# One encoder block on one core: rows of the first expert pair found by one-hot tables, expert weights loaded during the mix product, and more of the gated embedding inside the expert loop

## The chip, the core and the metric

The kernel runs on one core of a Trainium2 chip. The core has TensorE (PE in the profile, with its weight loads as PEld), VectorE (DVE), ScalarE (ACT), GpSimd (POOL) and SyncE (SP), and 16 DMA engines that all queues share. Time is device microseconds of one launch. One matrix product is meant by "product" below; "turned" means transposed on TensorE.

## What is computed

One transformer-like block over 512 tokens of width 1024, all in float32:

```python
h = _layernorm(x, ln0_w, ln0_b)
proj = h @ w_in[i]                       # q, k, v, z, xBC, dt, two gates
ya = _window_attention(...) @ w_out_attn[i]
ys = _ssd(...) @ w_out_ssd[i]
mix = (gates[:, :, 0, :] * ya + gates[:, :, 1, :] * ys) @ w_out[i]
h1 = _layernorm(DN_ALPHA * h + mix, ln1_w[i], ln1_b[i])
moe = _hier_moe(h1, ...)                 # 32 experts, the best 2 of the best group of 8
ple = jax.nn.sigmoid(h1 @ w_ple_gate[i] + b_ple_gate[i]) * (p[i] @ w_ple[i])
h = _layernorm(DN_ALPHA * h1 + moe + ple, ln2_w[i], ln2_b[i])
```

Every token goes to two experts with two weights. One expert is `silu(t @ w_gate) * (t @ w_up)`, weighted, times `w_down`; its three matrices have 1 MB each, so the 32 experts have 96 MB of weights. `ple` is the gated embedding.

## The kernel before

**Programs.** Each engine has one hand-written program, and semaphores join them; each engine does its work strictly in the order written. `link(...)` on VectorE makes the next instruction wait for the one before. `psum_plan` is a list of the units of work that need a PSUM bank, in TensorE's order; it gives each unit the next bank and the semaphore value at which the unit before in that bank has been read. `opened(key)` on TensorE is that wait. `plan_last` is the wait for all banks before the expert loop.

**Up to the expert loop.** The mix product (L1081) makes 8 bank-sized results in 55 us; VectorE adds and normalises each of the four token tiles (L1888, L1557 to L1572) and ScalarE scales them into `base`. TensorE turns `h1` (L1104) and makes the router's logits (L1096). VectorE picks group, two experts and their weights, then `sel` (which expert each token takes) and `upto` (running sums over the tiles). Meanwhile TensorE makes units of the gated embedding.

**The gated embedding** has 16 units `n` (four column slices by four token tiles). `ple_gate` is 8 accumulated products (L1125), `ple_in` two more (L1131). VectorE adds the bias (`ple_sum`, L1949), ScalarE takes the tanh (L1468), VectorE multiplies and adds to `base` (`ple_out`, L1956 and L1961). The first `EARLY` = 10 units come ahead of the loop, the other six in the loop, one for two pairs from pair 2 on, half a unit in each pair. ScalarE copies the turned rows of pair 0 behind the tanh of unit 8.

**The ranks and the rows.** Behind unit 1 TensorE sums `sel` to each token's rank within its expert (L1158 to L1160). From rank and count VectorE makes the row number of each choice (experts have 64 rows in order; what is over 64 goes to further rows, by a scan over the experts, L1990 and L1991) and then control words of the loop over full experts (L2013 to L2019), and storeU. POOL waits for the row numbers, scatters (weight, token) pairs to `row_info` in DRAM by 8 indirect DMAs (L769), loads the whole table back into `info` (L774), and then gathers the token rows of pair 0 and pair 1 (`rows_fetched`, L781).

**The expert loop.** 16 pairs of experts, 128 rows each (64 to an expert). For pair p TensorE does in this order: `gate_up` (L1180), turning of the rows of pair p+1 (L1145, ScalarE copies them), half of an embedding unit, `act_t` (L1205, ScalarE copies), the second part of the unit, `down` (L1195). ScalarE and VectorE copy the result to `eout`, and POOL scatters it to `y_rows` in DRAM (L801). There are two buffers `xg` for gathered rows, `xg[p % 2]`; POOL issues the gather of pair p+2 ahead of the scatter of pair p, which puts it right behind the scatter of pair p-1. The weights lie in a ring of 12 slots of 1 MB: slots 0 to 5 for even pairs, 6 to 11 for odd ones, each six being gate, up, down of one expert and then of the other. SP loads gate and up of pair p+2 when `gate_up` of pair p is done (L630), and down when `down` of pair p is done (L642).

**SP's order ahead of the loop.** After the second output product it loads one slice of the embedding's gate, then waits for the end of the mix product (`s_pe_mix`), and only then loads `w_ple`, all six slots of pair 0, stores `h1` to DRAM (L654), loads gate and up of pair 1, two more slices of the embedding gate (L617) and down of pair 1. `MOE_FREED` says for each slot which event frees it: the mix product for slots 0, 1, 8, 9, and the second output product (`s_pe_ys`, or `s_ys_read`) for the other eight.

**The end.** With pair 14's results in DRAM, POOL gathers each token's two rows with an adding DMA (L811), pair 15 is added by a product from chip memory (L1218), and VectorE, ScalarE and POOL normalise and store.

Of the kernel before, what the change touches and what calls it, by code (L numbers as in the profile page):

```python
# [113 lines left out]
EARLY = 10  # L114
LATE_FROM = 2
NO_TOKEN = 4 * ROWS

# [6 lines left out]
def psum_plan(sems):  # L124
# [89 lines left out]
    for n in range(EARLY):  # L214
        if n == EARLY - 1:
            for b in range(2):
                unit(("xf", b), 1, ("xgT_sb", b + 1))
        unit(("pl", n), 1, ("pp_read", n + 1))
        if n == RANKS_AFTER:
            unit("rk", 1, ("rk_read", 1))  # L220
# [15 lines left out]
    last = {}  # L236
    for b in range(8):
        for s, v in holder[b]:
            last[s.name] = (s, max(v, last.get(s.name, (s, 0))[1]))
    return place, list(last.values())  # L240


def block_kernel(nc, aps, out):
    with ExitStack() as ctx:
# [104 lines left out]
        xg = [shaped(R_A + 3072 + D * b, "p (k n) -> p k n", k=KD, n=P) for b in range(2)]  # L349
        xgT = [shaped(r, "p (k t) -> p k t", k=KD, t=P) for r in (R_X, R_A)]  # L350
        eactT = shaped(R_A + 1024, "p (b k t) -> p b k t", b=2, k=2, t=P)
        eout = shaped(R_Y, "p (b n) -> p b n", b=2, n=D)
# [42 lines left out]
        for c in range(2):  # L395
            rv[8 + c] = token_info[:, :, c, 0].bitcast(F32)
        storeU = ctx.enter_context(nc.sbuf_tensor("storeU", [P, PAIRS], U32))
        rowsU = ctx.enter_context(nc.sbuf_tensor("rowsU", [P, 2 * NT], U32))
        ctl = ctx.enter_context(nc.sbuf_tensor("ctl", [P, EXTRA + 2], I32))
# [37 lines left out]
        s_h1_ready = sem("h1_ready")  # L437
        s_h1_st = sem("h1_st")
# [62 lines left out]
        s_rk_read = sem("rk_read")  # L501
# [39 lines left out]
            s_rk_read, s_rt_read, s_sc_read, s_seg_read, s_st_read, s_xt_read, s_yT_read, s_ya_read,  # L541
# [6 lines left out]
        xg_in = [sem(f"xg_in{b}") for b in range(2)]  # L548
        plan, plan_last = psum_plan(sems)
# [43 lines left out]
        def _(sp):  # L593
# [25 lines left out]
            def gate_up_weights(p):  # L619

                for half in range(2):
                    for w, t in ((0, wg), (1, wu)):
# [4 lines left out]
                        elif half == w == 0:  # L627
                            sp.wait_ge(s_gu_mm, p - 1)
                        src = t[p * 2 + half].rearrange("(p k) f -> p k f", p=P)
                        sp.dma_start(ring[:, slot], src).then_inc(slot_in[slot], 16)  # L630

            def down_weights(p):

                for half in range(2):
                    slot = expert_slot(p % 2, half, 2)
# [50 lines left out]
        def _(pool):  # L686
# [90 lines left out]
            def rows_fetched(p):  # L777

                if p >= 2:
                    pool.wait_ge(s_xT_mm, 2 * (p - 1))  # L780
# [1366 lines left out]
```

## Time and profile before

| | |
|---|---|
| median of 3 runs | 821.24 us (820.75 to 822.28) |
| the profiled execution's own time | 820.64 us |
| its span in the trace | 818.6 us |
| TensorE busy / weight loads | 739.7 us (90%) / 499.5 us (61%) |
| VectorE, ScalarE, GpSimd busy | 403.5, 191.0, 162.2 us |
| DMA | 172.55 MB, 211 GB/s over the span |
| chain that ended last | PE 63%, DMA 23%, DVE 8% |

Times in the trace count from the span's start. A busy TensorE is not one at its peak, since products are pipelined. "The chain of waits" follows the work that ended last back from the end; its rows give start, duration and what ran, and a DMA's duration there is from its issue to its landing. In the timeline each row is one or several instructions of one engine in order of time: start, duration, engine, line, operation, output and inputs, and in brackets how long the engine had been idle and what released it. L numbers are lines of the kernel before.

### The profile page before, as it was taken

The numbers are of one execution on the slowest core, as the hardware profiler recorded it, in microseconds if no ns is written. First come the engines' busy times: TensorE is split into PE (matmuls) and PEld (weight loads), VectorE is DVE, ScalarE is ACT, GpSimd is POOL, SyncE is SP. The second block draws the span as 40 slices with busy tenths as digits, with TensorE's granted clock in tenths as the row PEclk, the third lists the DMA queues.
The fourth block names the chain that finished last, engine by engine and source line by source line (L and its number), as shares of the span: only waits on it lengthen the run. The fifth ranks groups of instructions, "written<-read, shape, count | busy, mean of one in ns | idle before, by whom it ended". The sixth has DMA issues, their size and how long they took to land.

```text
span 818.6 us, 9489 instructions
## 1 busy us (share of the span) xinstructions
PE 739.7 (90%) x3703; PEld 499.5 (61%) x3703; DVE 403.5 (49%) x742; ACT 191.0 (23%) x335; POOL 162.2 (20%) x117
## 2 busy tenths in 40 slices
PE   5999999999999999999999999689987989798761
PEld 2898789998888887558644698434443434343220
DVE  6598956677678888372245676111211102101217
ACT  4212424555232322410000241021211112111121
POOL 4924680000222240000000004101101100111152
PEclk9999999999999999999999999899999999999986
DMA  9797223111112141423220499179999999999592
GB/s 310 278 385 174 62 93 104 52 52 53 52 52 70 40 97 52 180 102 125 82 77 0 171 403 300 32 304 422 419 419 422 418 421 419 419 414 421 226 199 110
DMA packets 61814, 172.55 MB, mean 211 GB/s; under 512 B 17125, under 2 KB 39855, under 8 KB 47946
## 3 DMA queue, kind: packets, MB, share of 16 engines
q1 hardware_dynamic: 52324, 141.79, 45.9%
q0 software_dynamic: 8752, 28.01, 10.7%
q10 hardware_dynamic: 694, 2.14, 0.7%
q8 instruction: 31, 0.51, 0.3%
q14 instruction: 13, 0.11, 0.0%
HBM read 155.52 MB, written 24.67 MB: 220 GB/s over the span
## 4 chain that ended last, share of the span: by engine, by line
PE 63%; DMA 23%; DVE 8%; issue 2%; POOL 1%; SPq 1%; ACT 1%; POOLq 0%; DVEq 0%
PE psum L853 30%; DMA ring<-in_w_exp_up_dram 15%; PE psum L1180 9%; PE psum L1081 7%; PE psum L1062 3%; DMA ring<-in_w_in_dram 3%; PE psum L1195 2%; DMA arena<-y_rows,rowsU 2%; PE psum L1011 2%; PE psum L1031 1%; PE psum L961 1%; PE psum L1125 1%; PE psum L930 1%; DMA row_info<-token_info,rowsU 1%; PE psum L948 1%
## 5 line engine op out<-in xcount | busy, mean ns | idle before, releaser
L853 PE MATMUL psum<-ring_r 128*128 128x512 f32 (+1 forms) x832 | 215.4, 346 | 3.2 <-DVE arena_r L1597 1.7
L853 PEld LDWEIGHTS psum<-ring_r 128*128 128x128 f32 x832 | 146.2, 193 | 24.3 <-issue 3.0
L853 PE MATMUL psum<-arena_r,ring_r 128*128 128x512 f32 (+1 forms) x416 | 141.4, 377 | 0.0
L1180 PE MATMUL psum<-ring,arena 128*64 128x512 f32 x512 | 116.7, 609 | 21.8 <-DMA ring<-in_w_exp_up_dram 19.8
L1291 ACT COPY arena<-psum 128x512 f32<-128x512 f32 (+4 forms) x104 | 58.3, 578 | 243.0 <-PE psum L1088 110.6
L730 POOL TENSOR_TENSOR ring_r<-ring,ring_r 128x2048 fp32r<-128x2048 f32 x16 | 73.8, 4620 | 204.4 <-ACT ring_r L1291 204.4
L1180 PEld LDWEIGHTS psum<-ring,arena 128*64 128x64 f32 x512 | 42.9, 140 | 94.3 <-issue 92.0
L853 PEld LDWEIGHTS psum<-arena_r,ring_r 128*128 128x128 f32 x416 | 79.7, 192 | 13.7 <-issue 0.5
L2040 DVE SCALAR_TENSOR_TENSOR arena<-arena,psum 128x256 f32<-128x256 f32 x16 | 9.8, 612 | 131.4 <-ACT arena L1479 131.4
L1195 PE MATMUL psum<-ring,arena 128*64 128x512 f32 x256 | 62.5, 633 | 6.1 <-issue 5.6
L1125 PE MATMUL psum<-arena 128*128 128x256 f32 x256 | 60.5, 387 | 0.0
L801 POOL DMA_INDIRECT y_rows<-arena,storeU x15 | 15.0, 999 | 214.8 <-DVE arena L2071 214.8
L1081 PE MATMUL psum<-ring,arena 128*128 128x512 f32 x128 | 55.2, 593 | 1.6 <-DVE arena L1879 1.6
L1125 PEld LDWEIGHTS psum<-arena 128*128 128x128 f32 x256 | 48.6, 195 | 6.3
L1291 ACT CAST ring_r<-ring 128x2048 fp32r<-128x2048 f32 x22 | 41.8, 1899 | 15.1 <-DMA ring<-in_w_in_dram 12.8
L2071 DVE COPY arena<-psum 128x512 f32<-128x512 f32 x16 | 11.1, 692 | 68.6 <-PE psum L1195 68.6
L1081 PEld LDWEIGHTS psum<-ring,arena 128*128 128x128 f32 x128 | 24.2, 190 | 32.1 <-issue 30.1
L1195 PEld LDWEIGHTS psum<-ring,arena 128*64 128x64 f32 x256 | 19.8, 145 | 39.2 <-issue 39.2
L853 PE MATMUL psum<-ring_r,arena_r 128*128 128x256 f32 (+1 forms) x144 | 41.4, 295 | 0.0
L1479 ACT ACTIVATE arena<-psum 128x256 f32<-128x256 f32 x16 | 6.1, 384 | 128.0 <-PE psum L1180 128.0
L1062 PE MATMUL psum<-arena,ring 128*128 128x512 f32 x64 | 27.6, 592 | 0.0
L853 PEld LDWEIGHTS psum<-ring_r,arena_r 128*128 128x128 f32 (+1 forms) x144 | 26.1, 181 | 2.1
(272 smaller groups left out, 883.9 us busy)
## 6 DMA issues: line engine op xcount, KB each, us to landing
ring<-in_w_exp_gate_dram SPq DMA_DIRECT2D x32, 1024.0 KB, 17.3
ring<-in_w_exp_up_dram SPq DMA_DIRECT2D x32, 1024.0 KB, 20.1
ring<-in_w_exp_down_dram SPq DMA_DIRECT2D x32, 1024.0 KB, 20.7
ring<-in_w_in_dram SPq DMA_DIRECT2D x18, 1024.0 KB, 5.2
y_rows<-arena POOLq DMA_DIRECT2D x12, 1024.0 KB, 17.0
ring<-in_w_out_ssd_dram SPq DMA_DIRECT2D x4, 1024.0 KB, 6.5
ring<-in_w_out_dram SPq DMA_DIRECT2D x4, 1024.0 KB, 5.1
arena<-in_w_ple_gate_dram SPq DMA_DIRECT2D x4, 1024.0 KB
```

The source lines that it names most:

```text
L730: g.tensor_tensor(lo, ring[:, SLOT_OF[seq]], hi.bitcast(F32), ALU.subtract).then_inc(s_w_lo, 1)
L801: g.indirect_dma_start(out=y_dram, out_offset=bass.IndirectOffsetOnAxis(ap=storeU[:, p:p + 1], axis=0), in_=eout[:, p % 2, :], in_offset=N ...
L853: t = mm(o, a, b, start=(first and j == 0), stop=(last and j == 2))
L1011: t = mm(o[:, m * P:(m + 1) * P], dta[:, c, hh:hh + 1].broadcast_to([P, P]), upper, start=True, stop=True)
L1062: t = mm(o, ringN[:, s, j % 2, n * P:(n + 1) * P], yaT[:, j, :], start=(j == 0), stop=(j == 3))
L1081: t = mm(o, mixT[:, k, i * P:(i + 1) * P], ringN[:, s, k % 2, b * 512:(b + 1) * 512], start=(k == 0), stop=(k == KD - 1))
L1125: mm(ple_bank(n)[:, 0:PS], h1T[:, i, k, :], pgw[s][:, k, :], start=(k == 0), stop=(k == KD - 1))
L1180: t = mm(psum[sides[half], parity, :], xgT[parity][:, k, sides[half]], ring[:, s:s + 2, k, :], start=(k == 0), stop=(k == KD - 1))
L1195: t = mm(psum[sides[half], 4 + b, :], eactT[:, parity, k, sides[half]], ringN[:, s, k, b * 512:(b + 1) * 512], start=(k == 0), stop=(k == 1))
L1291: return nc.scalar.copy(dst, src)
L2040: v.scalar_tensor_tensor(e, by_k(eth[:, u % 2, :]), 1.0, by_k(hg), ALU.add, ALU.mult).then_inc(s_eact_a, 1)
L2071: v.tensor_copy(eout[:, u % 2, 512:1024], psum[:, 5, :]).then_inc(signal, 1)
```

## The change

Four things change together.

1. The row numbers are made twice. First without the overflow part: a choice of rank 64 or more gets a far row (`FAR`). Two tables `first_hot` say which of rows 0 to 127 each choice has, and eight small products of them with `tokw` (weight and token number as floats) give weight and token of each row of pair 0, without the way through DRAM. POOL gathers pair 0's rows by `first_token`, then does the scatter, the load of `info`, and pair 1's gather as before. The copy of the ranks out of PSUM and six steps for the number of further rows become direct reads and two instructions.
2. `xg` has one buffer instead of two. The gather of pair p+2 is issued behind the scatter of pair p, and waits until the rows of pair p+1 have been turned.
3. SP fills the eight slots that the second output product frees during the mix product, and `h1` tiles 0 to 2 are stored as they become ready.
4. `EARLY` is 5 instead of 10. The loop takes the other eleven units: three half units in pair 0 and one ahead of it, one unit in each of pairs 1 to 5, half a unit in each of pairs 6 to 13. `plan_last` is replaced by `freed(bank)` waits where a bank is first used.

The diff, cut to its core:

```diff
 RANKS_AFTER = 1
-EARLY = 10
-LATE_FROM = 2
+FIRST_AFTER = 2
+EARLY = 5
 NO_TOKEN = 4 * ROWS
+FAR = 4 * ROWS
+
+LATE = {0: (((5, 1),), ((6, 0),), ((6, 1),)), 1: (((7, 0),), (), ((7, 1),))}
+LATE.update({p: (((6 + p, 0),), ((6 + p, 1),), ()) for p in range(2, 6)})
+LATE.update({p: (((12 + (p - 6) // 2, p % 2),), (), ()) for p in range(6, 14)})
+
+
+def ple_done(p, *places):
+
+    return [n for place in places for n, half in LATE.get(p, ((), (), ()))[place] if half]
+
+
...
-        eout = shaped(R_Y, "p (b n) -> p b n", b=2, n=D)
...
+        eactT = shaped(R_A + 5632, "p (b k t) -> p b k t", b=2, k=2, t=P)
...
             sp.wait_ge(s_pe_ya, KD)
             gate_slice(1)
+            weights_in(0, (2, 3, 4, 5))
+            weights_in(1, (0, 1))
             sp.wait_ge(s_ys_read, KD)
             gate_slice(0)
+            weights_in(1, (4, 5))
+            for i in range(NT - 1):
+                sp.wait_ge(s_h1_ready, i + 1)
+                sp.dma_start(h1_dram[i * P:(i + 1) * P], h1_words[:, i, :]).then_inc(s_h1_st, 16)
             sp.wait_ge(s_pe_mix, 2 * NT)
...
-            gate_up_weights(0)
-            down_weights(0)
...
+            sp.wait_ge(s_h1_ready, NT)
+            sp.dma_start(h1_dram[3 * P:4 * P], h1_words[:, 3, :]).then_inc(s_h1_st, 16)
+            weights_in(1, (2, 3))
             sp.wait_ge(s_h1_st, 16 * NT)
             sp.wait_ge(s_ah1_ready, NT)
             sp.wait_ge(s_pe_h1T, NT)
             gate_slice(2)
...
             for p in range(2, PAIRS):
-                gate_up_weights(p)
-                down_weights(p)
+                sp.wait_ge(s_gu_mm, p - 1)
+                weights_in(p, (0, 1, 3, 4))
+                sp.wait_ge(s_y_mm, p - 1)
+                weights_in(p, (2, 5))
...
+
+                pool.wait_ge(s_xT_mm, 2 * p)
+                tokens = row_info[:, 2 * p + 1:2 * p + 2] if p else first_token[:, :]
+                g.indirect_dma_start(
+                    out=xg.rearrange("p k n -> p (k n)"), out_offset=None, in_=h1_dram,
+                    in_offset=bass.IndirectOffsetOnAxis(ap=tokens, axis=0),
+                    bounds_check=S - 1, oob_is_err=False).then_inc(s_xg_in, 16)
+
+            pool.wait_ge(s_h1_st, 16 * NT)
+            pool.wait_ge(s_first_read, 1)
+            rows_fetched(0)
+            pool.wait_ge(s_rows_ready, 1)
             for i in range(NT):
...
                     pool.wait_ge(s_pe_pl, 4 * NT)
...
+                if p + 2 <= LAST:
+                    rows_fetched(p + 2)
...
+                if half == 0:
+                    pe.wait_ge(pgw_in[s % 2], 16 * (s // 2 + 1))
+                    if n == EARLY:
+                        freed(6)
+                    elif n > EARLY:
+                        pe.wait_ge(s_pp_read, n)
+                for k in range(4 * half, 4 * half + 4):
                     mm(ple_bank(n)[:, 0:PS], h1T[:, i, k, :], pgw[s][:, k, :], start=(k == 0), stop=(k == KD - 1))
...
+                        t = mm(ple_bank(n)[:, PS:2 * PS], pT[:, k, i * P:(i + 1) * P], wple[:, k, PS * s:PS * (s + 1)],
+                               start=(k == 0), stop=(k == 1))
+                    t.then_inc(s_pe_pl, 1)
+
+            def rows_turned_in(p):
...
+                if n == FIRST_AFTER:
+                    pe.wait_ge(s_onehot_ready, 2)
+                    o = opened("first", 2)
+                    for i in range(NT):
+                        for c in range(2):
+                            t = mm(o, first_hot[c][:, i, :], tokw[:, i, c, :], start=(i == c == 0), stop=(i == NT - 1 and c == 1))
+                    t.then_inc(s_pe_rk, 1)
+            rows_turned_in(0)
+            ple_half(EARLY, 0)
 
...
                 q = p // 2
+                after_gate, after_act, after_down = LATE.get(p, ((), (), ()))
+                if p < 2:
+                    freed(p)
                 gate_up(q, p % 2, 2 * p + 2)
+                for n, half in after_gate:
+                    ple_half(n, half)
+                if 0 < p < LAST:
+                    rows_turned_in(p + 1)
                 if p == LAST:
                     break
-                rows_turned_in(p + 1, False)
-                late = EARLY + (p - LATE_FROM) // 2
-                late = late if p >= LATE_FROM and late < 4 * NT else None
-                if late is not None:
-                    if p % 2 == 0:
-                        pe.wait_ge(s_pp_read, late)
-                    ple_gate(late, range(4 * (p % 2), 4 * (p % 2) + 4))
+                if p == 0:
+                    freed(3, 4, 5)
                 act_t(p, p % 2, p, s_aT_mm)
-                if late is not None and p % 2:
-                    ple_in(late)
+                for n, half in after_act:
+                    ple_half(n, half)
                 if p == LAST - 1:
                     pe.wait_ge(s_last_rows, 1)
                     rows_turned(last_rows, s_last_rows)
                 down(p, q, p % 2, (s_aT_sb, p + 1), s_y_mm)
+                for n, half in after_down:
+                    ple_half(n, half)
+                if p == 0:
+                    rows_turned_in(1)
 
             pe.wait_ge(s_last_rows, 3)
...
-            for n in range(EARLY):
-                if n == EARLY - 1:
-                    rows_copy(0, 0, True)
+            for n in range(EARLY - 1):
                 ple_tanh(n)
+            rows_copy(0, 0, True)
+            ple_tanh(EARLY - 1)
...
+                if 0 < p < LAST:
+                    rows_copy(p + 1, (p + 1) % 2, False)
...
+
+            def rows_by_choice(out):
+
+                link(v.tensor_tensor(t5, t5, ranks, ALU.add))
+                link(v.tensor_tensor(t5, t5, per_e(first_row), ALU.add))
+                link(v.tensor_tensor(both, oh12, t5.unsqueeze(1).broadcast_to([P, 2, NT, NE]), ALU.mult))
+                link(v.tensor_reduce(out.rearrange("p i c -> p c i"), both, AX.X, ALU.add))
+
+            link(v.tensor_scalar(t5, ranks, float(CAP), float(FAR), ALU.is_ge, ALU.mult))
+            rows_by_choice(rowf)
+            for c in range(2):
+                v.tensor_tensor(first_hot[c], iota_c.unsqueeze(1).broadcast_to([P, NT, P]),
+                                rowf[:, :, c:c + 1].broadcast_to([P, NT, P]), ALU.is_equal).then_inc(s_onehot_ready, 1)
+
+            ple_sum(1)
+            ple_out(0)
+            more, csum = cnt[1], [cnt[2], cnt[3]]
+            steps_over = both.rearrange("p c i n -> p (c i n)")[:, 0:NE * (S // CAP - 1)].rearrange("p (e b) -> p e b", e=NE)
+            link(v.tensor_tensor(steps_over, count.unsqueeze(2).broadcast_to([P, NE, S // CAP - 1]),
+                                 above.unsqueeze(1).broadcast_to([P, NE, S // CAP - 1]), ALU.is_gt))
+            link(v.tensor_reduce(more, steps_over, AX.X, ALU.add))
...
+                                     ALU.is_gt))
+            dve.wait_ge(s_pe_rk, 2)
+            link(v.tensor_copy(first_w, bank("first", 1)))
+            v.tensor_copy(first_token[:, :], bank("first", 2)[:, 1:2]).then_inc(s_first_read, 1)
+            dve.wait_ge(s_first_read, seen(s_first_read))
...
+            link(v.scalar_tensor_tensor(t5, ranks, float(CAP), per_e(jump), ALU.is_ge, ALU.mult))
+            rows_by_choice(rowf)
+            v.tensor_copy(rowsU[:, :], rowf.rearrange("p i c -> p (i c)")).then_inc(s_rows_ready, 1)
+            dve.wait_ge(s_rows_ready, seen(s_rows_ready))
...
+            for n in range(2, EARLY):
+                ple_sum(n)
+                ple_out(n - 1)
+            ple_out(EARLY - 1)
...
                 v.tensor_copy(eout[:, u % 2, 512:1024], psum[:, 5, :]).then_inc(signal, 1)
 
-            dve.wait_ge(s_w_row, 16 * 2 * NT + 16)
             for p in range(PAIRS):
```
## Rows read from the trace of the kernel before

**Rows 1.** The page: the span, and what the DMA engines moved in 40 slices of it.

```profile
span 818.6 us, 9489 instructions
...
GB/s 310 278 385 174 62 93 104 52 52 53 52 52 70 40 97 52 180 102 125 82 77 0 171 403 300 32 304 422 419 419 422 418 421 419 419 414 421 226 199 110
```

**Rows 2.** The chain of waits around the loop's first pairs (start us, us, what).

```profile
502.09 7.42 DMA row_info<-token_info,rowsU
509.80 4.93 DMA info<-row_info
...
515.61 3.46 DMA arena<-h_rows,info
...
528.79 7.11 PE psum L1180 x32
...
542.46 6.88 PE psum L1180 x32
...
555.85 6.87 PE psum L1180 x32
```

**Rows 3.** The same chain later in the loop.

```profile
592.48 24.08 DMA ring<-in_w_exp_up_dram
616.80 7.10 PE psum L1180 x32
...
750.64 7.10 PE psum L1180 x32
...
761.77 0.70 DVE arena L2058
```

**Rows 4.** The timeline between the ranks and the first scatter of row numbers.

```profile
482.38 0.33 PE L1160 MATMUL psum<-arena 128*128 128x32 f32 x2
...
486.94 3.62 PE L1125 MATMUL psum<-arena 128*128 128x256 f32 x16
...
490.80 0.29 DVE L2008 TENSOR_REDUCE arena<-arena 128x4 f32<-128x128 f32 x1
...
491.98 0.17 DVE L2009 CAST rowsU<-arena 128x4 uint32<-128x4 f32 x1
...
493.01 1.09 POOL L769 DMA_INDIRECT row_info<-token_info,rowsU  x1 [87.16 <-DVE rowsU L2009]
...
496.53 0.17 DVE L2019 CAST ctl<-arena 128x17 int32<-128x17 f32 x1
```

**Rows 5.** The timeline of pair 5 in the loop, behind its gate and up product.

```profile
606.84 1.09 PE L1145 MATMUL psum<-arena 128*128 128x128 f32 x8
...
607.53 1.07 ACT L1291 COPY arena<-psum 128x512 f32<-128x512 f32 x2 [0.20 <-PE psum L1145]
...
607.77 1.89 PE L1125 MATMUL psum<-arena 128*128 128x256 f32 x8
...
609.72 1.03 PE L1131 MATMUL psum<-arena 128*128 128x256 f32 x4
...
610.67 3.65 PE L1195 MATMUL psum<-ring,arena 128*64 128x512 f32 x16
...
615.99 1.00 POOL L801 DMA_INDIRECT y_rows<-arena,storeU  x1 [13.72 <-DVE arena L2071]
...
617.29 1.01 POOL L781 DMA_INDIRECT arena<-h_rows,info  x1 [0.30 <-issue]
```

**Rows 6.** Single lines: the 16 gathers of token rows, issue to landing.

```profile
L781 POOL DMA_INDIRECT arena<-h_rows,info x16: 988/1014/1067, 515.6 to 736.1; - x16
...
DMA to landing us min/median/max: 3.3/10.2/11.7
```

**Rows 7.** The same of the 15 scatters of results.

```profile
L801 POOL DMA_INDIRECT y_rows<-arena,storeU x15: 997/997/1014, 544.0 to 770.0; - x15
...
DMA to landing us min/median/max: 4.6/8.3/10.0
```

**Rows 8.** The page: DMA issues of the LN1 weights (count, size, median to landing).

```profile
arena<-in_ln_w_dram POOLq DMA_DIRECT2D x2, 512.0 KB, 8.4
```

More of the change, by code:

```diff
@@ L214, in psum_plan @@
     for n in range(EARLY):
-        if n == EARLY - 1:
-            for b in range(2):
-                unit(("xf", b), 1, ("xgT_sb", b + 1))
         unit(("pl", n), 1, ("pp_read", n + 1))
         if n == RANKS_AFTER:
-            unit("rk", 1, ("rk_read", 1))
+            unit("rk", 1, ("rows_ready", 1))
+        if n == FIRST_AFTER:
+            unit("first", 1, ("first_read", 1))
+    for b in range(2):
+        unit(("xf", b), 1, ("xgT_sb", b + 1))
     place, holder, at = {}, [[] for _ in range(8)], 0
@@ L235, in psum_plan @@
         at += banks
[L236 to L240, printed above, removed]
+    return place, holder
 def block_kernel(nc, aps, out):
@@ L547, in block_kernel @@
         y_st = [sem(f"y_st{b}") for b in range(2)]
-        xg_in = [sem(f"xg_in{b}") for b in range(2)]
-        plan, plan_last = psum_plan(sems)
+        s_xg_in = sem("xg_in")
+        plan, holders = psum_plan(sems)
         def bank(key, n=512, banks=1):
@@ L826, in opened, with freed @@
                 return bank(key, n, banks)
+            def freed(*banks):
+                for b in banks:
+                    for s, v in holders[b]:
+                        pe.wait_ge(s, v)
             pe.wait_ge(s_consts, 4)
@@ L1965, in _ @@
             dve.wait_ge(s_bple_in, 16)
-            for n in range(RANKS_AFTER + 1):
-                ple_sum(n)
+            ple_sum(0)
             dve.wait_ge(s_pe_rk, 1)
-            rk = bank("rk", 160)
-            rank, count = t4, cnt[0]
-            link(v.tensor_copy(rank, rk[:, 0:128].rearrange("p (i n) -> p i n", i=NT)))
-            v.tensor_copy(count, rk[:, 128:160])\
-                .then_inc(s_rk_read, 1)
-            dve.wait_ge(s_rk_read, seen(s_rk_read))
-            dve.wait_ge(s_consts, 9)
+            dve.wait_ge(s_consts, 13)
@@ L1982, in _ @@
-                link(ins)
-            more, csum = cnt[1], [cnt[2], cnt[3]]
-            link(v.tensor_scalar(more, count, float(CAP), None, ALU.is_gt))
-            for b in range(2, S // CAP):
-                link(v.scalar_tensor_tensor(more, count, float(CAP * b), more, ALU.is_gt, ALU.add))
+                link(v.tensor_tensor(store_f[q], count[q, half:NE:2], row_of[q, half:half + 1].broadcast_to([CAP, PAIRS]),
+                                     ALU.is_gt))
+            dve.wait_ge(s_pe_rk, 2)
@@ L2078, in _ @@
                     break
-                late = EARLY + (p - LATE_FROM) // 2
-                if p >= LATE_FROM and p % 2 and late < 4 * NT:
-                    ple_sum(late)
-                    ple_out(late)
+                for n in ple_done(p, 0, 1):
+                    ple_sum(n)
+                    ple_out(n)
                 if p == LAST - 1:
```

153 lines of the change are left out of this document (61 added, 92 removed).

## Prediction

> **What bounds the kernel now.** I read first the page's slices. Counted from 0, slices 27 to 36 (553 to 757 us) show 414 to 422 GB/s without a break, slice 25 (512 to 532) shows 32 [rows 1]. So the expert loop is fed at the DMA engines' limit, and just ahead of it they stand still. The chain of waits says who holds them up: pair 0's first product starts at 528.79, behind the scatter of row numbers, the load of the table and the gather of the token rows [rows 2]. Later in the loop the chain alternates between a weight load that takes 24 us from issue to landing (it queues behind a whole pair of weights) and the product that waited for it [rows 3]. Pair 6 starts at 616.80 and pair 14 at 750.64: 133.84 / 8 = 16.73 us for a pair, which is the price of a pair's weights and rows. The first pairs ran faster, since TensorE alone set them: 13.4 us from pair 1 to pair 2 [rows 2]. What follows pair 14's start is an end of 818.6 - 750.64 = 68.0 us, which the change leaves as it is. So two questions decide: how much earlier do the weight loads of pair 2 and on begin, and does the loop keep a pace of 16.73?
>
> **Step 1, pair 0 starts earlier.** The rank product ends at 482.7 [rows 4]. VectorE then has a small copy and one bias add (about 0.6), three instructions of 128 columns at 0.29 and a gap of 0.03 [rows 4], two of 256 at about 0.45 (between the 0.29 of 128 columns and the 0.70 of 512 [rows 3]), and two of 512 at 0.70: 1.0 + 0.9 + 1.4 + 0.6 puts the tables at 486.6. TensorE is busy with unit 2 to 486.9 [rows 4] anyway. The eight small products are no rows here; one of 32 columns took 0.33 alone [rows 4] and cannot cost less than nothing, so they are 0 to 2.6 us, I take 2.0: 488.9. Two copies (0.4), POOL's start behind VectorE's signal (493.01 - 492.15 = 0.86 [rows 4]) and a gather with idle DMA engines (3.5 [rows 2]) land the rows at 493.7. That is hidden: units 3 and 4 keep TensorE to 497.5 (4.3 us for a unit: 1.73 twice and 0.95 less overlap, from 607.77 to 609.50 and 609.72 to 610.67 [rows 5]).
>
> What sets the start is ScalarE's order: the rows' copies stand behind the tanh of unit 3, and that behind VectorE. VectorE's second set of row numbers, some 20 small instructions, ends about 494.2; storeU, the 21 control instructions (492.15 to 496.70 = 4.55 [rows 4]), two bias adds and one output follow: 494.2 + 0.6 + 4.6 + 1.8 = 501.2. The tanh and two copies (0.5 + 1.3) give 503.0, and pair 0's product starts at about **503.2 instead of 528.79**, 25.6 us earlier. The filling of slots during the mix product costs nothing there and is needed: before, these loads kept the DMA engines busy until about 508 (slice 24, 491 to 512, still shows 300 GB/s [rows 1]), which would have held pair 0 by 5 us. It runs beside the loads of the LN1 weights, 8.4 us before [rows 8]; three times that, as the gathers show it under load (10.2 to 3.3 [rows 6]), would be 25 us, beside 55 us of mix products with only the last tile's norm on the path, so zero.
>
> **Step 2, pair 1.** The eight scatters now stand behind pair 0's gather and the second row numbers: POOL starts them at 495.1, the last 9.1 later at 504.2 (493.01 to 502.09 before [rows 2]). Landing 4.6 (a scatter with least load [rows 7]) to 7.4 [rows 2], table 4.9, next issue 0.9, gather 3.5 to 10.2 [rows 2, 6]: the rows are there between 518.1 and 527.6; I take 523. TensorE meanwhile: product 7.0, three half units 1.73 + 0.95 + 1.73 + 1.73 + 0.95, small turn 0.4, 1.1 of wait until unit 5 is out of its bank, down 3.65: 503.2 + 19.4 = 522.6. Turn and copies 1.9 (0.93, and the copies end 1.76 behind the turn's start [rows 5]): pair 1 at **525.0** (542.46 before). Its own round is 7.0 + 1.73 + 0.93 + 0.4 + 0.75 + 3.65 + 2.7 = 17.2: pair 2 at **542.2** (555.85 before). The lead has shrunk from 25.6 to 13.6.
>
> **Step 3, the rounds of pairs 2 to 5.** A whole unit in each, not half: gate and up 7.02, half unit 1.73, turn 0.93, small turn 0.22, the rest of the unit 2.68, down 3.65 [rows 5] (the 7.02 between the 6.87 and 7.11 of [rows 2]) = 16.2. The same round before, with its half unit only, was 1.7 shorter.
>
> Then the single buffer. Down of a pair ends at 614.32; the scatter starts 1.67 later and the gather 2.97 later (615.99, 617.29 [rows 5]). Before, this gather was for rows needed more than a round later. Now they are needed in this round, at 7.02 + 1.73 = 8.75 (9.7 where a half unit ends with the embedding's input part). Under load the gather takes 10.2 [rows 6], so it lands at 13.2, 4.4 or 3.5 late. Act_t, down, both result copies and POOL's next scatter are queued behind the turn. A round with a late gather is 13.2 + 0.93 + 0.4 + 2.6 + 3.65 = 20.8 in pairs 2 to 5. But a round of 20.8 gives the weights 4 us of pause, and with idle DMA engines the gather takes 3.3 to 3.5 [rows 2, 6] and is in time. So neither state lasts: rounds lie between 16.73 (weights) and the half-and-half of short and long, (16.2 + 20.8) / 2 = 18.5. I take 17.2, near the lower end, because at 17.2 the weights already pause 0.5 us a round, just between down's load and the next gate load, where the gather's last rows are due. Pair 6 at 542.2 + 4 x 17.2 = **611.0** (616.80 before).
>
> **Step 4, pairs 6 to 13.** Without a late gather 14.3 and 15.9 (half a unit; in odd pairs ScalarE's tanh stands ahead of act_copy), mean 15.1; with one 13.2 + 1.76 + 0.8 + 3.65 = 19.4. The mean of both is 17.25, the weights' floor 16.73, the largest 17.9; I take 17.35: pair 14 at 611.0 + 138.8 = **749.8**, against 750.64. In pair 14 the turn of pair 15 may be 3.5 late before it matters, since down waits for VectorE's tables until 762.5 [rows 3].
>
> Sum: -0.8 on the profiled execution's own 820.64, which stands 0.6 under the median of 821.24: **820.5**. The 25.6 us won at pair 0 are spent: 12 on the first two pairs (the way through DRAM now stands there, and three half units), 8 in pairs 2 to 5 (moved units, late gathers), 5 in pairs 6 to 13 (late gathers).
>
> On sharing the DMA engines, the row says 10.2 us under load against 3.3 [rows 6], a factor of three. The Trainium skill ("DMA: Bandwidth & Descriptors", Queues, rings and completion order) says each engine takes turns between the queues it has work for, a whole packet from one before the next. With turns of equal size a gather would take at most twice its idle time. By that rule the first rival below would hold; the rows of before speak against equal turns.
>
> **Rivals.** *A, the gather is not late.* If the gather of the new order takes at most twice 3.5, it lands at 2.97 + 7.0 = 10.0, and costs at most about 1 us in a round. Then the weights set the loop: gate of pair 4 is issued at 542.2 + 7.1 = 549.3, pair 14's lands ten rounds and two thirds later, 549.3 + 1 + 10.67 x 16.73 = 728.8, and the time is 21.8 lower, about 799.5. For it: the DMA engines idle in rounds 0 to 2, so the loop enters without a queue. Against: half of the 16 gathers took 10.2 or more, and one 11.7 [rows 6].
>
> *B, slower: gathers are late in more than every second round.* If a pair's weights spill into the next round's scatter and gather whenever a round is near 17, rounds 2 to 5 take 18.5 and 6 to 13 take 17.9: pair 14 at 542.2 + 74 + 143.2 = 759.4, time 830. It decides from a mean round of 17.4 over pairs 2 to 13 on ((750.6 - 542.2) / 12). For it: 16.2 and 16.73 lie so near each other that there is nothing to spare; 11.7 instead of 10.2 adds 1.5 to each late round.
>
> *C, pair 1's rows come late.* The load of the table is issued about 509 and pair 2's weights start at 510.3; if it takes twice its 4.9 beside them and the gather 10.2, pair 1 starts some 7 us later and everything behind it too: 827.
>
> **How the numbers follow.** My forecast 0.48 (own range 815 to 826), A 0.24, B 0.20, C 0.08. Two tenths of a per cent, 1.6 us, is what a measurement of this kernel tells from no change. Faster: A 0.24 and 0.16 of mine; within it: 0.17 of mine and 0.01 of C; slower: B 0.20, C 0.07 and 0.15 of mine. The range leaves out the best part of A and the worst of B: 804 to 831.
>
> **What would show it.** Step 1: the first L1180 product at 503 +- 3, behind ScalarE's copies. Step 2: the second at 525, with or without a wait of TensorE for the gather. Step 3 and 4: a wait of the turning behind the gather's DMA, of 3 to 4 us, in about every second round, gathers of both 4 and 10 us, and DMA slices that show less than 420 GB/s from 550 on. I am wrong if no such wait shows (A), if it shows in each round (B), or if the start of pair 0 has another releaser than the copies.

## The result, and the profile after

The kernel after the change takes **837.16 us** (median of 4 runs, 835.77 to 838.96), the kernel before, run beside it, 821.25. The ratio is 1.0177, with a 95% interval of 1.0154 to 1.0200: slower by 15.9 us. The forecast was 820.5, in a range of 804 to 831.

The page of the kernel after, with the lines that answer to [rows 1] and the granted clock of TensorE in the same 40 slices (20.9 us each):

```profile
span 836.2 us, 9526 instructions
...
PEclk9999999999999999999999999999998988989885
...
GB/s 306 286 375 155 99 75 80 51 52 51 55 49 100 51 51 64 163 150 102 235 318 50 285 118 153 314 392 365 364 339 346 397 316 417 338 368 362 172 182 121
```

Before, ten slices in a row moved 414 to 422 GB/s. Now the loop's slices lie between 314 and 417: the weights have stopped setting its pace. The clock of TensorE drops to 8 tenths and back in several slices of the loop. The chain of waits says what sets the pace instead (start, duration, what; for a DMA the duration runs from issue to landing):

```profile
504.83 8.64 PE psum L1211 x32
...
528.19 7.09 PE psum L1211 x32
...
565.75 7.86 DMA arena<-h_rows,info
...
584.10 6.54 DMA arena<-h_rows,info
...
601.12 9.72 DMA arena<-h_rows,info
610.88 1.97 PE psum L1169 x8
...
656.53 1.00 POOL y_rows L813
657.84 10.92 DMA arena<-h_rows,info
668.80 1.97 PE psum L1169 x8
671.20 0.68 issue
671.88 5.32 PE psum L1226 x16
...
678.76 1.00 POOL y_rows L813
680.07 6.96 DMA arena<-h_rows,info
687.08 1.09 PE psum L1169 x8
688.39 1.24 issue
689.63 3.67 PE psum L1226 x16
```

L1211 is the gate and up product, L1169 the turning of the token rows, L1226 the down product, L813 the scatter of results. The weight loads of [rows 3] have left the chain. In their place stands the gather behind the scatter, in every round from pair 2 to pair 14 but those of pairs 7 and 13, and TensorE turns the rows about 0.04 us after they land. From pair 8 on gathers of 9.4 to 10.9 us and of 6.8 to 7.3 us take turns; before that they took 9.48, 7.86, 6.54, 9.72, 7.89 and 6.5. After the one issued at 657.84 the turning takes 1.97 us instead of 1.09 and down 5.32 instead of 3.67.

The windows over this stretch (length, busy time of TensorE, its weight loads, VectorE, ScalarE and GpSimd, then granted clock, DMA share, GB/s) show what the clock did:

```profile
657.00:668.00 11.00, 6.70 (x32) 3.01 (x27) 1.27 (x2) 0.38 (x1) 1.55 (x2) 1.00 1.02 408
668.00:678.00 10.00, 8.52 (x32) 4.17 (x34) 0.69 (x1) 2.03 (x4) 0.00 (x0) 0.66 0.72 303
678.00:684.00 6.00, 6.00 (x31) 1.88 (x27) 0.00 (x0) 0.00 (x0) 2.03 (x2) 1.00 0.92 344
684.00:694.00 10.00, 8.52 (x46) 5.08 (x46) 3.16 (x6) 2.62 (x6) 0.00 (x0) 1.00 0.99 364
```

TensorE waits 5.11 us for the rows that land at 668.8. The granted clock, 1.00 until then, is 0.66 over the next ten microseconds: part of them at 1.2 GHz instead of 2.4. The DMA engines meanwhile have less to do (0.72 busy, 303 GB/s), and the next gather takes less time (6.96). Of the waits of TensorE for a DMA between 500 and 790 us all are of this kind (in total, times, longest); none is for weights:

```profile
PEld psum L1169 <- DMA arena<-h_rows,info: 35.0, 12, 7.1
PE psum L1169 <- DMA arena<-h_rows,info: 29.7, 11, 6.2
```

Beside them TensorE stands idle for 3.0 us ahead of pair 0's product, 8.6 in nine pieces ahead of down, and 2.5 for VectorE and ScalarE.

### The profile page after: what moved, and what is told of

It is laid out like the page before. It is cut to its first block, busy times and chain, and to the rows that moved or that the text cites. A ratio compares the mean times of both kernels' runs of the same rounds, so it can differ in the third digit from the quotient of the medians.

```text
span 836.2 us, 9526 instructions
## 1 busy us (share of the span) xinstructions
PE 751.3 (90%) x3719; PEld 503.5 (60%) x3719; DVE 406.3 (49%) x740; ACT 189.4 (23%) x335; POOL 163.1 (20%) x121
## 4 chain that ended last, share of the span: by engine, by line
PE 69%; DMA 17%; DVE 6%; issue 4%; POOL 2%; ACT 1%; SPq 0%; POOLq 0%; DVEq 0%
PE psum L873 30%; DMA arena<-h_rows,info 12%; PE psum L1226 7%; PE psum L1101 7%; PE psum L1150 5%; PE psum L1211 4%; PE psum L1082 3%; DMA ring<-in_w_in_dram 3%; PE psum L1169 2%; DMA arena<-y_rows,rowsU 2%; PE psum L1031 2%; PE psum L1051 1%; POOL y_rows L813 1%; PE psum L1153 1%; PE psum L981 1%
## 5 line engine op out<-in xcount | busy, mean ns | idle before, releaser
L1211 PE MATMUL psum<-ring,arena 128*64 128x512 f32 x512 | 114.4, 599 | 4.2 <-issue 3.0
L1211 PEld LDWEIGHTS psum<-ring,arena 128*64 128x64 f32 x512 | 40.1, 139 | 74.5 <-issue 73.1
L1226 PE MATMUL psum<-ring,arena 128*64 128x512 f32 x256 | 67.2, 672 | 9.3 <-issue 9.3
L1150 PE MATMUL psum<-arena 128*128 128x256 f32 x256 | 63.7, 396 | 1.4 <-DVE arena L1998 1.4
L813 POOL DMA_INDIRECT y_rows<-arena,storeU x15 | 15.1, 1007 | 239.0 <-DVE arena L2116 239.0
L1150 PEld LDWEIGHTS psum<-arena 128*128 128x128 f32 x256 | 48.2, 196 | 20.5 <-issue 14.6
L2116 DVE COPY arena<-psum 128x512 f32<-128x512 f32 x16 | 11.1, 692 | 99.8 <-PE psum L1226 99.8
L1226 PEld LDWEIGHTS psum<-ring,arena 128*64 128x64 f32 x256 | 20.8, 154 | 46.8 <-issue 46.8
L1169 PE MATMUL psum<-arena 128*128 128x128 f32 x128 | 22.1, 330 | 29.7 <-DMA arena<-h_rows,info 29.7
L1326 ACT CAST ring_r<-ring 128x2048 fp32r<-128x2048 f32 x22 | 41.8, 1899 | 15.3 <-DMA ring<-in_w_in_dram 12.9
L1169 PEld LDWEIGHTS psum<-arena 128*128 128x128 f32 x128 | 17.9, 168 | 35.5 <-DMA arena<-h_rows,info 35.0
```

Source lines behind the costliest of these rows:

```text
L813: g.indirect_dma_start(out=y_dram, out_offset=bass.IndirectOffsetOnAxis(ap=storeU[:, p:p + 1], axis=0), in_=eout[:, p % 2, :], in_offset=N ...
L1150: mm(ple_bank(n)[:, 0:PS], h1T[:, i, k, :], pgw[s][:, k, :], start=(k == 0), stop=(k == KD - 1))
L1169: t = tr(o[:, k * P:(k + 1) * P], xg[:, 4 * b + k, :], ident)
L1211: t = mm(psum[sides[half], parity, :], xgT[parity][:, k, sides[half]], ring[:, s:s + 2, k, :], start=(k == 0), stop=(k == KD - 1))
L1226: t = mm(psum[sides[half], 4 + b, :], eactT[:, parity, k, sides[half]], ringN[:, s, k, b * 512:(b + 1) * 512], start=(k == 0), stop=(k == 1))
L1326: return nc.scalar.copy(dst, src)
```

## The experiments

Each was compared with the kernel before on the same chip (823.07 in the runs of the first four, 821.55 in those of the next four, 821.88 in the last three). "After" in a diff is the changed kernel. Medians are given first, then the ratio to before with its interval. The first four ran on one chip and the other seven on another, so a difference of medians between those two groups holds 1.2 to 1.5 us that the kernel before shows as well; where it matters, the ratios are compared.

**The order of GpSimd's two issues.** One buffer still, but the gather of pair p + 2 is issued as soon as the rows of pair p + 1 are turned, ahead of the scatter of pair p.

```diff
-                if p == LAST - 1:
+                if p + 2 <= LAST:
+                    rows_fetched(p + 2)
+                else:
...
-                if p + 2 <= LAST:
-                    rows_fetched(p + 2)
```

> The changed kernel, with POOL's gather of pair p+2 issued ahead of the scatter of pair p (its wait is for the turning of pair p+1's rows, which is done before down of pair p); still one buffer. Theory (the gather behind the scatter lands after its rows are needed, and that alone sets the rounds): the gather starts some 5 us earlier in the round and is in time at 10 us, the rounds of pairs 2 to 13 fall from 18.8 to the weights' 16.7 to 17, pair 14 starts near 735 instead of 768, time 801 to 808. Rival (the moved embedding units and the weights fill the round, the gather is only what is seen waiting): rounds stay above 18, time 825 to 838.

Measured: **805.16 us** (ratio 0.9775, 0.9750 to 0.9800), 32.0 below after. Between 500 and 790 us no wait of TensorE for token rows is left. One for weights is back:

```profile
PE psum L1211 <- DMA ring<-in_w_exp_up_dram: 4.6, 3, 2.7
```

Pair 14 starts at 736.02 (768.01 in after). The whole of the loss, and more, hung on the place of one issue in GpSimd's order. Every other part of the change stayed in. Where nothing waits, a round of this kernel takes 16.06 us in pairs 3 to 5, 14.44 to 14.48 in pairs 6, 8 and 10, and 15.64 and 15.65 in pairs 7 and 9.

**Two buffers.** After, with a second buffer for odd pairs from pair 3 on, and gathers issued a round ahead.

```diff
-        xg = shaped(R_A, "p (k n) -> p k n", k=KD, n=P)
+        xg = [shaped(r, "p (k n) -> p k n", k=KD, n=P) for r in (R_A, R_Y)]
...
+                if 2 <= p and p + 2 <= LAST:
+                    rows_fetched(p + 2)
```

> The changed kernel with a second buffer for the rows of pairs 3, 5, 7 and so on (in the space that the second slice of the embedding's gate leaves after pair 1), so that from pair 4 on a gather is issued a round ahead, behind the scatter of the pair before, as in the kernel before. Theory: no wait for rows, rounds set by the weights, time 801 to 808, within 3 of the run with the gather ahead of the scatter. Rival (a late gather is not the cause): 825 to 838.

Measured: **803.66 us** (0.9764, 0.9737 to 0.9791), 1.5 from the run before it, within both intervals. So the buffer's number is not the matter: one buffer does as well if its gather starts early.

**The same loss alone, on the kernel before.** Its two buffers are made one, with the gather behind the scatter; nothing else.

```diff
-        xg = [shaped(R_A + 3072 + D * b, "p (k n) -> p k n", k=KD, n=P) for b in range(2)]
+        xg = shaped(R_A + 3072, "p (k n) -> p k n", k=KD, n=P)
...
-                if p >= 2:
-                    pool.wait_ge(s_xT_mm, 2 * (p - 1))
+                pool.wait_ge(s_xT_mm, 2 * p)
...
-                if p + 2 <= LAST:
-                    rows_fetched(p + 2)
-                else:
+                if p == LAST - 1:
...
+                if p + 2 <= LAST:
+                    rows_fetched(p + 2)
```

> The kernel before with only the second part of the change: one buffer for gathered rows, the gather of pair p+2 behind the scatter of pair p. Theory: the wait for rows comes in about every second round, rounds of pairs 1 to 13 go from 16.0 to about 18.5, so the time rises by 25 to 40, to 846 to 861. Rival (the single buffer only hurts together with whole units in the loop): at most 5 us slower than 821.

Measured: **873.19 us** (1.0599, 1.0572 to 1.0627), 50 to 52 us lost, more than was expected. The chain shows the same picture as in after:

```profile
583.71 10.50 DMA arena<-h_rows,info
594.21 0.04 issue
594.25 1.97 PE psum L1144 x8
596.22 2.28 PE psum L1124 x8
...
606.12 6.33 DMA arena<-h_rows,info
612.46 0.04 issue
612.50 1.09 PE psum L1144 x8
613.60 1.73 PE psum L1124 x8
```

Here too the work right behind a long gather ran slower: the turning 1.97 instead of 1.09 us and the half unit of the embedding 2.28 instead of 1.73; down, in this round, did not (3.61). The waits for rows sum to 55.8 us between 500 and 790, of which 5.6, ahead of pair 0, are in the kernel before as well (6.1). So this part of the change loses as much and more without the others.

**The clock.** After, with 24 turnings of the identity (2.78 us) ahead of each wait for rows in pairs 2 to 14. They write a bank part that nothing reads.

```diff
+FILL = 24
...
+                if 2 <= p < LAST:
+                    for _ in range(FILL):
+                        tr(psum[:, 3, 256:384], ident, ident)
```

> The changed kernel with 24 turns of the identity (2.6 us, into an unused half of bank 3) ahead of the wait for rows in pairs 2 to 14. Theory on the length of the long rounds (21 to 22 us where 19.4 was forecast: TensorE's granted clock falls after the wait): with the wait filled the mean of a down product falls from 5.5 back to 3.7 us in the long rounds and the granted clock is 1.00 there, the short rounds grow by up to 2.6; time 828 to 840. Rival (the clock has no part in it): down products stay at 5.3 to 5.7 in long rounds, and the time rises by 5 to 15.

Measured: **841.34 us** (1.0222, 1.0197 to 1.0247). The granted clock of the loop's slices now reads 9, and a late gather finds TensorE at speed (a gather of 10.20 us, landing 693.88):

```profile
683.63 10.20 DMA arena<-h_rows,info
...
693.88 1.09 PE psum L1170 x8
...
696.43 3.65 PE psum L1227 x16
```

All 13 turnings take 1.04 to 1.34, and 12 of 13 downs 3.65. One took 5.28 behind a wait of only 0.68; why is not settled. The clock's part is what was expected, and the time is 1.3 over the expected 828 to 840. The sum explains it: 13 times 2.78 is 36.1 put in, the waits for rows fell from 29.7 to 7.6, and the slow turnings and downs of pairs 2 to 13 of after (turnings over 1.09: 0.88 three times, 0.72, 0.67; downs over 3.65: 2.03, 1.66, 2.08, 1.63) were 11 us and one more turning of 0.88 in pair 14, 12 in all, now gone. 36.1 - 22.1 - 12 = +2; the spans say 839.0 against 836.2. So the clock cost about 12 us in after, and buying it back this way costs as much as it gives.

**Slot filling.** The first experiment's kernel, with the sync engine's old order: the weights of pairs 0 and 1 as in the kernel before, and `h1` stored behind those of pair 0.

```diff
-            weights_in(0, (2, 3, 4, 5))
-            weights_in(1, (0, 1))
...
+            weights_in(0, (0, 1, 3, 4))
+            weights_in(0, (2, 5))
...
+            weights_in(1, (0, 1, 3, 4))
...
+            weights_in(1, (2, 5))
```

> The run with the gather ahead of the scatter, with SP's order of the kernel before (no slot filled during the mix product, h1 stored after pair 0's slots). Theory of the prediction: the loads keep the DMA engines busy to 508, pair 0 starts at 508 to 510, and the scatters land later; time 808 to 813. Rival (nothing but pair 0 feels it and the loop's weights absorb it): 804 to 806.

Measured: **813.78 us** (0.9896, 0.9869 to 0.9922), 8.6 above the first experiment, 9.9 by the ratios; by the spans (811.2 and 805.2) 6.0. The timeline shows where:

```profile
503.92 7.09 PE L1208 MATMUL psum<-ring,arena 128*64 128x512 f32 x32 [1.51 <-issue]
...
512.89 1.49 POOL L797 DMA_DIRECT2D info<-row_info  x1 [6.46 <-DMA row_info<-token_info,rowsU]
...
523.08 1.05 POOL L781 DMA_INDIRECT arena<-h_rows,info  x1 [8.70 <-DMA info<-row_info]
531.50 1.57 PEld L1166 LDWEIGHTS psum<-arena 128*128 128x128 f32 x8 [8.19 <-DMA arena<-h_rows,info]
```

Pair 0 is not held (508 to 510 was expected). The weight loads lie on the way of pair 1's row numbers: the scatters land late, and the table's load is issued at 512.89 instead of 508.9, now behind pair 2's first weights (511.04). It lets GpSimd wait 8.70 us, TensorE waits 7.79 for the gather behind it, and pair 1 begins at 534.24 instead of 529.68.

**Pair 0's rows from the small product.** The first experiment's kernel, with pair 0's gather put behind the table in DRAM again.

```diff
-                tokens = row_info[:, 2 * p + 1:2 * p + 2] if p else first_token[:, :]
+                tokens = row_info[:, 2 * p + 1:2 * p + 2]
...
-            pool.wait_ge(s_h1_st, 16 * NT)
-            pool.wait_ge(s_first_read, 1)
-            rows_fetched(0)
...
+            pool.wait_ge(s_h1_st, 16 * NT)
+            rows_fetched(0)
```

> The run with the gather ahead of the scatter, with pair 0's rows gathered by the table from DRAM as before (behind the eight scatters and the load of the table, together with pair 1's); the tables, the small product and pair 0's weights from it stay. Theory: pair 0 starts at 519 to 522 instead of 505 and pair 1 at 540 to 544 instead of 530; of those 10 to 14 us the later rounds, which TensorE sets at 16.1 and 15.1, give back little: time 812 to 818. Rival (weights set the end anyway): 805 to 808.

Measured: **820.38 us** (0.9988, 0.9970 to 1.0005), 15.2 above the first experiment (17.5 by the ratios, 15.3 by the spans), and over the expected 812 to 818. TensorE waits 18.08 us for these rows, and pair 1 begins at 544.35, 14.7 later than there. That is this part's worth: 15 us at pair 1, kept to pair 14 (750.62 against 736.02).

**Earlier copies.** The first experiment's kernel, with ScalarE's copies of pair 0's rows behind the tanh of unit 1 instead of unit 3.

```diff
-            for n in range(EARLY - 1):
+            for n in range(2):
...
-            ple_tanh(EARLY - 1)
+            for n in range(2, EARLY):
+                ple_tanh(n)
```

> The run with the gather ahead of the scatter, and ScalarE's copies of pair 0's turned rows put behind the tanh of unit 1 instead of unit 3. Theory of step 1 (ScalarE's order, behind VectorE's control instructions, sets pair 0's start): pair 0's gate and up product starts at 501 to 502 instead of 505, and since TensorE no longer stands 3 us it takes 7 us and not 10; pair 1 starts 3 to 6 us earlier, time 798 to 802 against 805. Rival (pair 1's rows or the weights hold it anyway): pair 0 earlier, time unchanged within 1.5.

Measured: **809.24 us** (0.9837, 0.9819 to 0.9855), 4.1 above the first experiment (2.4 by the spans) and not 3 to 7 below it. Pair 0 did start at 500.50 (504.98 in the first experiment), but pair 1 at 529.64, as there (529.68), and its product ran at the lower clock (8.64 us) behind a wait of 6.61 for the rows. The timeline, with the sync engine's first load of pair 2's weights (which waits for pair 0's gate product) between the table's load and its use:

```profile
507.61 1.49 POOL L800 DMA_DIRECT2D info<-row_info  x1 [1.43 <-DMA row_info<-token_info,rowsU]
...
507.78 0.34 SPq L645 DMA_DIRECT2D ring<-in_w_exp_gate_dram  x1
...
518.10 1.05 POOL L784 DMA_INDIRECT arena<-h_rows,info  x1 [9.00 <-DMA info<-row_info]
```

The weights were issued 0.17 us behind the table's load, which then took 9.71 us (4.93 in [rows 2]); the gather behind it took 8.76. This is the mechanism of rival C. It does not act in after, where the weights were issued at 513.50 and the table's load at 508.75.

**The same with two buffers.** The second experiment's kernel with the same move of the copies.

> The run with two buffers and ScalarE's copies of pair 0's rows behind the tanh of unit 1: the version in which rows are never late. Theory: 798 to 801, and at or below the run with one buffer and the same copies; rounds 4 to 12 as there. Rival: the end waits for the weights, 802 to 804.

Measured: **809.98 us** (0.9855, 0.9835 to 0.9875). The same loss by the same wait (5.97 us for pair 1's rows), where 798 to 801 was expected: the buffers have no part in it.

**The weights held back.** The kernel with the earlier copies, in which the sync engine's first load of pair 2 waits until pair 1's rows have landed.

```diff
+            sp.wait_ge(s_xg_in, 32)
```

> The run with the copies of pair 0's rows put earlier and the gather ahead of the scatter, and SP's first load of pair 2's weights held until the rows of pair 1 have landed. Theory (the load of the table and the gather of pair 1 take twice and three times as long beside pair 2's weights, which pair 0's end lets go): the table takes 5 us again and not 9.8, pair 1's rows land about 517 instead of 527 and pair 1 starts at 522 to 523 instead of 529.6; time 796 to 801. Rival (the weights held back are missed in pair 2 and after): pair 1 at 522, but a wait for weights at pair 2 or 3, time 803 to 809.

Measured: **802.25 us** (0.9752, 0.9727 to 0.9776), 7.0 below the kernel without that wait. The time falls between the expected 796 to 801 and the rival's 803 to 809. The same rows of its timeline:

```profile
509.01 1.49 POOL L801 DMA_DIRECT2D info<-row_info  x1 [1.43 <-DMA row_info<-token_info,rowsU]
...
514.47 1.05 POOL L785 DMA_INDIRECT arena<-h_rows,info  x1 [3.97 <-DMA info<-row_info]
...
518.00 0.34 SPq L645 DMA_DIRECT2D ring<-in_w_exp_gate_dram  x1
```

GpSimd waits 3.97 us for the table instead of 9.00, and pair 1 begins at 523.78, 5.9 earlier than in the first experiment. Of that lead 3.0 is left at pair 14 (733.04 against 736.02): this kernel waits for weights again from pair 11 on, the first experiment's from pair 12 on.

**That with two buffers.**

> The same with two buffers for gathered rows. Theory: as the run with one buffer, 796 to 801, since one buffer costs nothing once the gather goes ahead of the scatter. Rival: 2 us or more apart.

Measured: **802.18 us** (0.9747, 0.9716 to 0.9777), no different from one buffer. Both are some 3 us below the first experiment by the medians, but their intervals overlap with its.

**Is the moved work of the embedding dear?** The first experiment's kernel, in which units 8 to 11 leave out three of the eight gate products (so its output is not the reference's), 1.3 us less for TensorE in each of pairs 2 to 5.

```diff
+                    if 8 <= n < 12 and 4 <= k < 7:
+                        continue
```

> The run with the gather ahead of the scatter, which leaves out three of the eight gate products of the embedding's units 8 to 11 (the second halves in pairs 2 to 5), so its output is not the reference's. Theory (moved units cost nothing once the rows are in time, for the weights come at 16.7 a pair at best): the rounds of pairs 2 to 5 fall from 16.1 to 14.8, waits for weights grow by the same later, time 803 to 806. Rival (TensorE sets the loop): 800, by 4 times 1.3 us faster.

Measured: **802.94 us** (0.9762, 0.9732 to 0.9792), 2.2 below the first experiment by the medians, but with overlapping intervals, just below the expected 803 to 806; the rival had 800. From pair 1 to pair 8 it takes 106.62 us (525.62 to 632.24) instead of 111.78, the whole 5.2 saved. From pair 8 to pair 14 it takes 99.06 instead of 94.56, since TensorE is back at waiting for weights sooner, from pair 9 on; up to the loop's end it waits 10.9 us for them, instead of 4.6:

```profile
PE psum L1213 <- DMA ring<-in_w_exp_up_dram: 10.9, 6, 3.7
```

So 4.5 of the 5.2 is paid back to the weights. Pair 1 began 4.1 earlier in this run than in the first experiment's profiled one, 2.9 of it because TensorE's clock was up in pair 0's product (7.09 us against 9.97); the edit has no part in those 4.1. Of the lead of 4.7 at pair 14 it accounts for 0.7: once the rows are in time, 5.2 us of TensorE's work in pairs 2 to 5 are worth that much.

## Why the prediction was wrong

**Step 1 held.** The small product of the tables ended at 490.46 (488.9 forecast) and took 1.68 (2.0). Pair 0 started at 504.83 (503.2), its rows' copies behind the tanh of unit 3, as the forecast said; moving them brought it to 500.50, so ScalarE's order did set it. Most of the 1.6 that it started late is the clock again. The first product of the embedding, ahead of the ranks, took 5.39 us instead of 3.70, and the rank product ended at 484.38 instead of 482.7. The lines are that product and the window over it, first before, then after:

```profile
473.24 3.70 PE L1125 MATMUL psum<-arena 128*128 128x256 f32 x16
...
473.00:479.00 6.00, 6.00 (x31) 5.33 (x31) 4.80 (x21) 5.53 (x3) 0.00 (x0) 1.00 1.02 403
...
473.23 5.39 PE L1150 MATMUL psum<-arena 128*128 128x256 f32 x16
...
473.00:479.00 6.00, 6.00 (x23) 4.99 (x23) 4.81 (x21) 5.50 (x3) 0.00 (x0) 0.72 0.70 281
```

Among the profiled runs with these copies and pair 0's rows from the small product, where this embedding product took 3.70, pair 0 started at 503.78 to 503.92; where it took 5.28 or 5.39, at 504.83 to 505.24. With the earlier copies it was 500.12 and 500.50, and 501.31 and 501.97. So by like against like, moving the copies is worth 3 to 4 us and not 4.5. Why the clock was lower there is open: the waits of TensorE just ahead (0.32 and 0.6 us) are the same in both kernels. The work during the mix products cost them nothing: they took 55.20 us in both. That slot filling saves 5 us was near in size (6 to 10) and wrong in place: the old order holds pair 1's row numbers, not pair 0.

**Step 2 held but for one term.** Pair 1 started at 528.19 (525.0) and pair 2 at 545.61 (542.2). The 3.4 us are 1.6 from pair 0's start, 1.6 from its product, 8.64 instead of 7.0, and 0.2 from pair 1's round. TensorE had stood idle for 3.02 us before that product, and the granted clock from 505 to 514 was 0.83; where the product ran at full clock (501.97 in the kernel with the weights held back), pair 0 to pair 1 took 21.81 us, and the forecast had 21.8.

**Steps 3 and 4 failed, in the size of a round and not in its kind.** The forecast named the wait (turning behind the gather, DMA slices under 420 GB/s), and that is what the trace shows. It took 17.2 for a mean round of pairs 2 to 5 and 17.35 for pairs 6 to 13. Measured were 18.5 ((619.61 - 545.61) / 4) and 18.55 ((768.01 - 619.61) / 8). With the 3.4 of step 2 that puts pair 14 at 768.01 instead of 749.8, and the end behind it took 68.2 (68.0). Round by round, with TensorE's wait for the rows (us):

| pair | 2 | 3 | 4 | 5 | 6 | 7 | 8 | 9 | 10 | 11 | 12 | 13 |
|---|---|---|---|---|---|---|---|---|---|---|---|---|
| round | 17.02 | 18.35 | 17.02 | 21.61 | 19.47 | 15.63 | 22.29 | 16.09 | 21.03 | 16.43 | 21.57 | 15.89 |
| wait | 0.69 | 2.07 | 0.75 | 3.92 | 2.10 | - | 5.11 | 0.24 | 3.63 | 0.59 | 4.41 | - |

Where the 5.2 us over in pairs 2 to 5 and the 9.6 over in pairs 6 to 13 come from:

- **Pairs 6 to 13: the clock, a cost that the forecast did not have.** A late round was put at 19.4. The four late ones took a mean of 21.1, though on the average the wait in them was no longer than forecast: the rows landed 11.1, 14.1, 12.6 and 13.4 us into the round, mean 12.8 (13.2). The forecast let TensorE come out of its wait at full speed. In these four rounds the turning and down took 2.5 to 2.8 us longer than at full clock, 10.5 together. The run with filled waits shows that the clock is the cause. That run did not get faster, so what the rounds would take with the clock for nothing was not measured.
- **Pairs 6 to 13: the rounds in time.** The forecast had 14.3 for an even round in time and 15.9 for an odd one, and reckoned with their mean, 15.1. But the four in time were all odd, and took 15.6 to 16.4, mean 16.0: the price of an odd round was right. With 15.9 beside its 19.4 its own mean would have been 17.65 instead of 17.35, 2.4 us more over the eight rounds.
- **Pairs 2 to 5: the balance.** The forecast chose 17.2, since any longer round would give the weights a pause and the gather behind it only 3.3 to 3.5 us. No gather behind these scatters took less than 6.5. The scatter and the gather are issued right behind the loads of down's weights (677.21, 678.76 and 680.07), with the DMA engines 0.92 busy; that this is the reason is argued and not tested. So TensorE waited in each of these four rounds, 7.4 us in all, where 17.2 leaves room for 4; another 1.4 went to the clock in pair 5. Without waits the other three took 16.3 (16.2 forecast). The mean is the 18.5 that the forecast named as the largest, but not by its half-and-half: one round of 21.6 stands beside three of 17.0 to 18.4.

Of the forecast's working one figure has no source: the 17.9 called the largest mean of pairs 6 to 13, on which rival B's 830 rests too. It was exceeded (18.55).

**The rivals.** A fell: it needed gathers of at most 7.0 us, and they took 6.5 to 10.9. The rule of turns between queues by whole packets (the Trainium skill, "DMA: Bandwidth & Descriptors", Queues, rings and completion order) would, with equal turns, have allowed twice the idle 3.3. The runs show 2.0 to 3.3 times the idle time. B had the right side and, for pairs 2 to 5, the right number (18.5) and its condition, waits in more than every second round: TensorE waited in all four of them and in pair 6, and in 11 of the 13 rounds from pair 2 to pair 14. From pair 7 on the waits over 1 us came in every second round only, and B's 17.9 falls short by the clock. C did not happen in after (TensorE did not wait for pair 1's rows), and was shown at once when pair 0 was brought 4.5 us forward.

**Where the gain went.** 24.0 us earlier at pair 0 (528.79 to 504.83), 14.3 at pair 1, 10.2 at pair 2; then 17.4 later at pair 14 (750.64 to 768.01). With the gather ahead of the scatter it is 14.6 earlier at pair 14, and 13.4 at the end of the span (818.6 to 805.2; 17.9 by the medians of that comparison).

## What to carry to other kernels

When a double buffer is given up, ask first where the next load now stands in its queue and what it waits behind; here the issue's place was worth 32 us and the second buffer 1.5 at most. Price a wait of TensorE with what runs after it: in this loop a wait of 2 us and more was mostly followed by turnings or down products at the lower clock, which took 1.4 to 1.8 times as long. A stage brought forward triggers its successors' loads earlier too; hold a bulk load back when a short chain of small transfers is still under way beside it.

## What the runs showed of the hardware

- Waits of TensorE of 0.04 to 0.75 us in after were followed by turnings at 1.09 us and downs at 3.65. Of seven waits of 2.07 to 6.21 us, six were followed by turnings of 1.76 to 1.97, and four by downs of 5.28 to 5.73; the one of 2.07 by neither.
- An idle time of 3.0 to 3.1 us ahead of pair 0's product was followed by 8.48 to 9.97 us for it in three kernels (after, gather ahead, filled waits) and by 7.09 in two (two buffers, the lighter units). In the three the embedding's first product had run slow as well (5.28 or 5.39), in the two it had not (3.70).
- A load of the small table took 4.93 us with idle DMA engines and 9.71 when weight loads were issued 0.17 us behind it. A gather of 128 rows took 3.3 us idle and 6.5 to 10.9 in the loop.
- In the kernel with the gather ahead, the loop ran at 419 to 421 GB/s from 600 us to pair 14, as before the change, and still took only 14.4 to 16.1 us a round from pair 3 to pair 10, less than the 16.73 of a pair's weights before. That fits a lead of loaded weights, won in the first rounds, that lasts for that long.
